# Triangular inverses in a hybrid encoder step: level products beside another tile's update products

## What is computed

```
L = jnp.where(strict, beta[..., None] * kk * decay, 0.0)
A = L + jnp.eye(T, dtype=L.dtype)
sol = lax.linalg.triangular_solve(A, rhs, left_side=True, lower=True, unit_diagonal=True)
u, w = sol[..., :GDN_DV], sol[..., GDN_DV:]
v_new = u - jnp.einsum('bhtk,bhkv->bhtv', w, S)
```

## Time and profile before

| | us |
|---|---|
| median of three runs | 961.93 (960.17 to 962.16) |
| the profiled execution | 960.13, with a span of 958.4 |
| PE busy in the span | 944.0 (99%) |
| DVE, ACT, POOL busy | 647.2, 443.5, 169.8 |

### The profile page before, as it was taken

The page is one execution under the profiler, slowest core; times in us unless marked ns, Lnnn a source line. Parts: engine busy times, 40 slices in busy tenths (PEclk is TensorE's granted clock), DMA queues, the critical chain, the costliest instruction groups (busy, mean ns, idle before and its releaser), DMA issues.

```text
span 958.4 us, 16641 instructions
## 1 busy us (share of the span) xinstructions
PE 944.0 (99%) x6807; PEld 856.8 (89%) x6807; DVE 647.2 (68%) x1083; ACT 443.5 (46%) x813; POOL 169.8 (18%) x198
## 2 busy tenths in 40 slices
PE   8999999999999999999999999999999999999998
PEld 7899889998998877879878999999999999888887
DVE  7627887876665454671665899999999999435321
ACT  6633455648533345463654354444444446323310
POOL 0061101104654232000000142222222220000000
PEclk9999999999999999999999999999999999999999
DMA  8724242211104056143831432222222223413221
GB/s 299 236 72 143 85 137 89 87 54 45 44 4 133 1 188 204 46 154 110 314 126 47 165 121 67 79 78 87 88 88 90 88 88 111 184 38 117 64 102 55
DMA packets 73820, 103.69 MB, mean 108 GB/s; under 512 B 2577, under 2 KB 53905, under 8 KB 73361
## 3 DMA queue, kind: packets, MB, share of 16 engines
q1 hardware_dynamic: 73744, 102.63, 31.9%
HBM read 92.27 MB, written 10.35 MB: 107 GB/s over the span
## 4 chain that ended last, share of the span: by engine, by line
PE 89%; DVE 5%; ACT 3%; issue 1%; POOL 1%; DMA 1%; SPq 0%; ACTq 0%; DVEq 0%; POOLq 0%
PE bank L1178 8%; PE bank L1177 8%; PE bank L1176 8%; PE bank L520 7%; PE bank L521 7%; PE bank L522 7%; PE bank L493 6%; PE bank L495 5%; PE bank L494 5%; PE bank L461 4%; PE bank L813 2%; PE bank L546 2%; PE bank L548 2%; PE bank L547 2%; PE bank L575 1%
## 5 line engine op out<-in xcount | busy, mean ns | idle before, releaser
L2119 DVE TENSOR_TENSOR wlo<-wraw,whi 128x2048 fp32r<-128x2048 f32 (+1 forms) x56 | 126.1, 2253 | 103.8 <-ACT whi L1569 94.4
L1569 ACT ACTIVATE whi<-wraw 128x2048 fp32r<-128x2048 f32 (+1 forms) x58 | 109.3, 1885 | 100.0 <-PE bank L522 72.8
L493 PE MATMUL bank<-hhi,whi 128*128 128x320 f32 x352 | 115.8, 329 | 0.0
L495 PE MATMUL bank<-hhi,wlo 128*128 128x320 f32 x352 | 108.8, 309 | 0.0
L494 PE MATMUL bank<-hlo,whi 128*128 128x320 f32 x352 | 108.7, 309 | 0.0
L493 PEld LDWEIGHTS bank<-hhi,whi 128*128 128x128 f32 x352 | 66.2, 188 | 4.5 <-issue 3.8
L494 PEld LDWEIGHTS bank<-hlo,whi 128*128 128x128 f32 x352 | 66.2, 188 | 2.8 <-issue 2.2
L495 PEld LDWEIGHTS bank<-hhi,wlo 128*128 128x128 f32 x352 | 66.1, 188 | 0.0
L520 PE MATMUL bank<-whi,hhi 128*128 128x512 f32 x150 | 58.4, 389 | 0.0
L521 PE MATMUL bank<-wlo,hhi 128*128 128x512 f32 x150 | 58.4, 389 | 0.0
L522 PE MATMUL bank<-whi,hlo 128*128 128x512 f32 x150 | 58.3, 389 | 0.0
(11 more groups left out here) (489 smaller groups left out, 2667.4 us busy)
## 6 DMA issues: line engine op xcount, KB each, us to landing
wraw<-in_w_in SPq DMA_DIRECT2D x13, 1024.0 KB, 5.3
wraw<-in_w_gate SPq DMA_DIRECT2D x11, 1024.0 KB, 5.2
wraw<-in_w_up SPq DMA_DIRECT2D x11, 1024.0 KB, 5.2
wraw<-in_w_down SPq DMA_DIRECT2D x10, 1024.0 KB, 5.2
kTs<-in_cache_sb_k SPq DMA_DIRECT2D x8, 512.0 KB, 4.4
vraw<-in_cache_sb_v SPq DMA_DIRECT2D x8, 512.0 KB, 5.0
wraw<-in_w_mix_out SPq DMA_DIRECT2D x4, 1024.0 KB, 6.2
kmT<-in_cache_mem_k SPq DMA_DIRECT2D x8, 512.0 KB, 6.2
```

The source lines that it names most:

```text
L493: T.matmul(o, wh[:, k, cs], hhi[:, k, hs], start=(k == 0), stop=False)
L495: ins = T.matmul(o, wl[:, k, cs], hhi[:, k, hs], start=False, stop=(k == KD - 1))
L1569: V(wv(whi, i), wv(wraw, i), ACT.Copy).then_inc(s["w_hi_ready"], 1)
L2119: V.tensor_tensor(wv(wlo, i), wv(wraw, i), wv(whi, i).bitcast(F32), ALU.subtract)\
```

## The change

The two kinds of product share steps. At step n, PE issues Y of entry n and dX of entry n - 2 (`LAG = 2`) of one list, head by head. Y is now written to the other half of the partitions, so that it lies on the off-diagonal quadrants of the array, while dX stays on the diagonal ones. ACT, which copies Y into `Xb`, therefore moves each half across, with two copies of [64 x 256]. The list `LM_ORDER` takes the sample tile one level late, at the end of a round (rounds of 4, 5, 5, 5 and 4 entries). Two fill units are cut in halves of 12 matmuls, put behind steps 1, 7, 12 and 17; so one fill goes from before the stage into it. Behind the stage the transposes of v and k of the sample tile and a fill stand ahead of the level-6 transposes, and those of tile 0 ahead of the level-6 products. On DVE the first four `turn_blocks` go into the tile loop, and the sB products are spread over the stage. On ACT the copies of Y come before Silu, and the cut of the weight block before the last `blocks_out`. POOL makes four `lmb` in its tile loop; the ring has 12 buffers. `Xb` and `lmb` get other addresses.

```diff
-LM_RING = 10
+LM_RING = 12
-        Xb = [at(f"Xb{n}", [P, HEADS, BLOCK], R0 + TILE * (7, 7, 9, 9, 5)[n] + BT * (n % 2 if n < PT else 1)) for n in range(NT)]
-        lmb = [at(f"lmb{n}", [P, HEADS, BLOCK], CQ + BT * ((n + 8) % LM_RING)) for n in range(LM_RING)]
+        Xb = [at(f"Xb{n}", [P, HEADS, BLOCK], MEMV - 4096 + BT * n if n < PT else R0 + TILE * 5 + BT) for n in range(NT)]
+        lmb = [at(f"lmb{n}", [P, HEADS, BLOCK], MEMV + BT * n if n < PT else CQ + BT * (n - PT)) for n in range(LM_RING)]
-        LM_ORDER = [(l, i) for l in range(1, LEVELS - 1) for i in TILES_AT[l]]
+        LM_ORDER = [(l, i) if i < PT else (l - 1, i) for l in range(1, LEVELS - 1)
+                    for i in (range(NT) if 1 < l <= SAMPLE_LEVELS else range(PT))]
+        LAG = 2
+        HALF_FILLS = (1, 7, 12, 17)
...
             fill()
-            fill()
             pe.wait_ge(s["silu_done"], 12)
+            def level_products(n):
+                y = dx = None
+                if n < len(LM_ORDER):
+                    l, i = LM_ORDER[n]
+                    pe.wait_ge(s["lm_ready"], n + 1)
+                    pe.wait_ge(s["xb_ready"], n + 1)
+                    y = packed(take(("Y", l, i)))
+                if n >= LAG:
+                    l2, i2 = LM_ORDER[n - LAG]
+                    evacuated(pe, ("Y", l2, i2))
+                    dx = packed(take(("dX", l2, i2)))
                 for h in range(HEADS):
+                    if y is not None:
+                        for g in range(2):
+                            last_y = T.matmul(y[half64(1 - g), h, :], lmb[n % LM_RING][half64(g), h, :],
+                                              Xb[i][half64(g), h, :], start=True, stop=True)
+                        if h == HEADS - 1:
+                            done(last_y, ("Y", l, i))
+                    if dx is not None:
+                        for g in range(2):
+                            last_dx = T.matmul(dx[half64(g), h, :], Xb[i2][half64(g), h, :], XTb[i2][half64(g), h, :],
+                                               start=True, stop=True)
+                        if h == HEADS - 1:
+                            done(last_dx, ("dX", l2, i2))
...
+            for n in range(len(LM_ORDER) + LAG):
+                level_products(n)
+                if n in HALF_FILLS:
+                    half_fill()
+
+            turn_vk(PT)
+            fill()
             upper, lower = half64(0), half64(1)
...
-            turn_vk(PT)
-            fill()
+            turn_vk(0)
...
-            turn_vk(0)
...
-                if i < 2:
+                if i < PT:
                     level_mask(i)
-            for n in range(2, len(LM_ORDER)):
+            for n in range(PT, len(LM_ORDER)):
...
+            cut_hi(B_OUT[0][0])
             blocks_out(PT)
 
+            for l, i in LM_ORDER:
+                b = filled(e, ("Y", l, i))
+                for g in range(2):
+                    ins = V(Xb[i][half64(g), :, :], packed(b)[half64(1 - g), :, :], ACT.Copy)
+                ins.then_inc(bank_free[b], 1)
             evacuated(e, (("z", 1), 1, 1))
             for j in range(4):
                 V(qkvz[:, 12 + j, :], qkvz[:, 12 + j, :], ACT.Silu)
             e.preload_act_table_set(LN_EXP)
-            for l in range(1, LEVELS - 1):
-                for i in TILES_AT[l]:
-                    b = filled(e, ("Y", l, i))
-                    V(Xb[i][:, :, :], packed(b), ACT.Copy).then_inc(bank_free[b], 1)
-                if l == 4:
-                    cut_hi(B_OUT[0][0])
...
+            def turn_blocks(i, first=True):
+                if first:
+                    dve.wait_ge(s["xt0_ready"], i + 1)
+                V.transpose(flat(Xb[i]), flat(XTb[i])).then_inc(s["xb_ready"], 1)
...
+                if i >= 1:
+                    turn_blocks(i - 1)
...
             gate_yb(0, 0)
-            gate_yb(0, 1)
-
-            for l in range(1, LEVELS - 1):
-                if l == 1:
+
+            for n, (l, i) in enumerate(LM_ORDER):
+                if n == PT:
+                    turn_blocks(PT)
+                if n == 8:
+                    gate_yb(0, 1)
+                if n == 18:
                     gate_yb(1, 0)
```

More of the change, by code:

```diff
@@ L408, in hybrid_step @@
         N_S = 2 * PT
-        TILES_AT = [list(range(NT)) if l < SAMPLE_LEVELS else list(range(PT)) for l in range(LEVELS)]
         GN = (4, 5, 6, 7, 0, 1, 2, 3)
@@ L484, in across_half, with unit @@
                     ends[i] = ("bank", (name, 1, 1))
-            def unit(name, i, c, h, at="bulk"):
-                if c == 0 and h == 0:
+            def unit(name, i, c, h, at="bulk", ks=range(KD)):
+                if c == 0 and h == 0 and ks[0] == 0:
                     lo_cut(pe, i)
@@ L490, in unit @@
                 hs, cs = slice(h * HALF, (h + 1) * HALF), slice(c * P, (c + 1) * P)
-                o = bank[take((name, c, h), at=at)][:, 0:HALF]
-                for k in range(KD):
+                o = bank[take((name, c, h), at=at) if ks[0] == 0 else use[name, c, h][0]][:, 0:HALF]
+                for k in ks:
                     T.matmul(o, wh[:, k, cs], hhi[:, k, hs], start=(k == 0), stop=False)
@@ L495, in unit @@
                     ins = T.matmul(o, wl[:, k, cs], hhi[:, k, hs], start=False, stop=(k == KD - 1))
+                if ks[-1] < KD - 1:
+                    return
                 done(ins, (name, c, h))
@@ L503, in fill, with half_fill @@
                 unit(*next(fills), at="few")
+            halved = []
+            def half_fill():
+                if not halved:
+                    halved.append(next(fills))
+                    unit(*halved[0], at="few", ks=range(KD // 2))
+                else:
+                    unit(*halved.pop(), at="few", ks=range(KD // 2, KD))
             def down(name, half, blks, left, tiles, ready=None, behind=lambda i: None, cut=lo_cut):
@@ L806, in _ @@
             fill()
-            fill()
             pe.wait_ge(s["silu_done"], 12)
-            def by_block(b, left, right):
-                for h in range(HEADS):
[L812 to L815, removed]
+            def level_products(n):
[9 more added lines that the diff above has]
+                    dx = packed(take(("dX", l2, i2)))
+                for h in range(HEADS):
+                    if y is not None:
[10 more added lines that the diff above has]
+                            done(last_dx, ("dX", l2, i2))
             def turn_vk(i):
@@ L2393, in vk_part @@
                     .then_inc(bank_free[b], 1)
[L2395 to L2400, removed]
-            gate_yb(0, 0)
-            gate_yb(0, 1)
-            for l in range(1, LEVELS - 1):
-                if l == 1:
-                    gate_yb(1, 0)
[L2407 to L2418, removed]
+            gate_yb(0, 0)
+            for n, (l, i) in enumerate(LM_ORDER):
[4 more added lines that the diff above has]
+                if n == 18:
+                    gate_yb(1, 0)
+                b = filled(dve, ("dX", l, i))
+                if l < last_level(i):
+                    V.tensor_tensor(XTb[i][:, :, :], XTb[i][:, :, :], packed(b), ALU.subtract).then_inc(bank_free[b], 1)
+                    evacuated(dve, ("dX", l, i))
+                    turn_blocks(i, first=False)
+                    continue
+                dve.wait_ge(s["xt_zero"], 1)
+                for g in range(2):
+                    ins = V.tensor_tensor(XT[i][half64(g), :, half64(g)], XTb[i][half64(g), :, :], packed(b)[half64(g), :, :],
+                                          ALU.subtract)
+                ins.then_inc(bank_free[b], 1)
             vk_part(PT)
```

## The result

The changed kernel takes 955.38 us (median, 955.26 to 956.03), the kernel before in the same rounds 961.21. The ratio is 0.9942 with a 95% interval of 0.9929 to 0.9954: 4.4 to 6.8 us faster, and on the forecast of 955.4. From profiled execution to profiled execution it is 960.13 to 955.39, 4.7 us. The two differences are not the same, for a reason found only in the runs: the kernel before takes 960.0 to 961.0 us in executions with a mean granted clock of 0.999 or 1.00 and 961.6 to 962.8 in those with 0.998 (13 and 7 of the 20 in one group of runs), while all nine executions of the changed kernel have 0.999 or 1.00.

The account below looks back on a forecast made before the run. PE, busy 99% at full clock, was taken as the bound. Savings of 4.9 us in the stage and 1.6 behind it made 6.5: 953.6 us from the profiled 960.13, 955.4 from the median 961.93; range 953.3 to 957.6.

Parts of the forecast that it names:

- the mechanism: Shared steps on PE: 32 records on four quadrants take 0.49 us, both products in the time of one.
- The rivals: Shared step slower on PE: 0.98 us (chance 0.13), 0.70 us (0.14), or 2.0 us (0.07 with other slower ways).
- what sets the pace: Inside the stage: round trips over ACT, 1.66 us for two steps, and DVE, 1.69 us, decide, not PE.
- The stage: Shared steps, four half units and last two steps: 26.8 us against 31.7, 4.9 saved.
- The stretch behind: From the stage's end to `w_part`: 11.5 us instead of 13.1, 1.6 saved.
- The sum of both: Stage and stretch behind it: 4.9 + 1.6 = 6.5 us less.
- The lower end of my range: Whole kernel: 953.3 us; the stage's own low end, all returns cheaper by 0.1, was 25 us.
- Silu: On ACT behind Y's copies: its 5.2 us covered by 5.5 us of other work; loss of perhaps 0.5 if not.
- The falling clock: Granted clock falls while PE waits in every step; chance 0.07 together with rival 3 and other slower ways.

Follow-up runs that it names:

- the diagonal experiment: Changed kernel with Y put back on the diagonal quadrants, so ACT needs one copy again: 957.21 us, ratio 0.9960 to the kernel before.
- short copies: Changed kernel with ACT's copies of Y cut to one head of four, leaving part of the computation out: 953.16 us, ratio 0.9916 to the kernel before.

## Why the prediction was right, and where its sum was off

**Right: the mechanism.** Four quadrants run at once. The 32 records of a shared step take 0.47 to 0.48 us, as L1111's rate in the earlier trace rows suggested (8 repeats of the 58 ns above are 0.47), with Y and dX of one half on the same rows of the array. By the rule of the Trainium skill that a weight load overlaps with matmuls in flight only where the row group differs (TensorE: Matmul & The Clock Gate, "The mechanism"), two products that share their rows would have run two quadrants at a time, 0.93 us as in the step of the diagonal experiment; the trace disagrees. Nor does the floor of about 25 ns show that the Trainium skill gives on the same page ("Back-to-back issue gap"): 32 records in 0.47 us are 15 ns each. The rivals, which all built on slower records, fall.

**Right: what sets the pace, a little short.** I had 1.66 us for ACT's trip and measured 1.74. The way from the start of the step to ACT's copy takes 0.73 us (269.69 to 270.42), not 0.68, and the return from ACT to PE 0.24 (chain, 285.08), not 0.14 plus 0.05; that 0.05 I had from no row. Over the stage this is 0.6 us (21 steps at 0.87 instead of 0.84).

**The stage was 2.2 us too short in my sum,** 26.8 against 29.0 us (258.65 to 287.68), and it began 0.15 us later. Besides the trip: five steps with a half unit take 6.07 us, so that the half costs 1.72 (6.07 - 5 x 0.87), where I had 1.61 (1.96 - 0.35); times four 0.4 us. And 0.88 us is PE's stop in step 7, of which I had allowed nothing although show one of 0.75 in the stage before. Some 0.3 us lie in the first two steps and the last two.

**The cause of that stop stays open.** It comes again at the same place in a second run (266.58), and in the one with the old order behind the stage (266.88), shorter with Silu first (0.64) and with short copies (0.46), and not at all with Y on the diagonal or Y and dX in turn. One candidate is in the traces. In the seven profiles with a stop of this kind (0.75 us in the kernel before and with the order alone, step 7 of the changed kernel twice, of the old order, Silu first and short copies) PE goes on 1.2 to 1.6 us after a packet of 16 KB has landed on the DMA queue that the profile calls `instruction`; in the changed kernel the packet is under way from 265.0 to 266.0 us and PE goes on at 267.53. Such packets come every few us, most of them with no stop behind them, and no run here tests it, so this is not shown.

**The stretch behind gave 0.7 us more,** 2.3 instead of 1.6 us, with 10.9 against a sum of 11.5: the second product of level 6 takes 1.73 us (296.25 to 297.98) instead of 2.0, the fill 3.51 (288.70 to 292.21) instead of 3.72, the transposes 1.01 instead of 1.2, the wait for the last copy 0.56 instead of 0.75; those of v and k take 0.1 more each. The experiment with the order alone confirms the term, 13.2 to 10.9.

**The sum of both, 6.5 us, was 1.8 more than the 4.7 of the profiled spans,** and the median still fell on the forecast. For the profiled execution I had 953.6 us, and it took 955.39. The forecast of 955.4 started from a median of 961.93 us, which lies among the executions of the kernel before at a clock of 0.998; these take 1.4 to 1.9 us more than its others. The runs fit that they vanish with the new order behind the stage: none in the 15 executions of the changed kernel and of the one with the order alone, two of five with the old order on the changed kernel, where the trace shows the dip. That the dip lies there in the kernel before as well is inferred, since its profiled execution had none. So the term for the stage was too large by 2.4 us, a gain behind it and one in the clock that I had not seen made up for it, and the close hit is in part luck. The lower end of my range does not follow from my own sum: a stage of 25 us gives 953.6 us, not 953.3; nothing hangs on it.

**Silu** fitted: its 5.2 us behind the copies cost nothing visible, and ACT waits 0.4 us for the level-6 transposes. The falling clock I had among the slower ways; it did not come in the changed kernel, but it did in two variants that let PE wait longer inside the stage.

## What to carry to other kernels

When a change makes the bound engine twice as fast in a stage, work out the round trip over the other engines first: here it left 0.06 us a step, between half units, of a possible 0.47. What the faster engine then has to spare is worth nothing until other work is cut to the size of its waits; quarters in place of halves, and one unit more of them, gave 3.8 us on top of 5.8. Two equal times do not say that a difference is worth nothing: look whether a stop that one variant has and the other has not covers it. And where two releasers end close together, shorten one of them to see which is the true one, since the table of waits names only the later.

## What the runs showed of the hardware

Matmuls of 64 x 64 on all four quadrants, Y and dX sharing rows in pairs, start 15 ns apart on the mean, 29 with both products on the same two quadrants (diagonal, 64 in 1.86 us) and 23 to 24 with all of Y ahead of all of dX (0.72 to 0.77 us for 32); alone on a quadrant they took 62 (L853, 32 in 2.00 us). TensorE's granted clock fell to half after stretches with PE busy 1.80 of 4 us (lag 3), 0.73 of 3 us (Silu first) and 1.24 of 2 us (old order), and did not fall in the changed kernel. An ACT copy of 64 partitions x 256 takes 0.38 us, as one of 128 x 256 does; with 64 columns it takes 0.22.
